# Two transformer-like blocks on one core: rope by pairs of heads, the delta rule's moment, low halves and rope tables in another order

## The chip, the cores and the metric

One core of a Trainium2 chip runs the whole program. The metric is the device time in microseconds. The kernel before took 2430.34 us (median of 3 runs, 2429.22 to 2437.76). The profiled execution took 2433.86 us, with a span of 2432.1 us from the first to the last instruction.

## The reference

The program computes a first block of 2 layers (l = 0, 1) and then a second block of 2 layers on an input of 256 rows by 1024 columns, all in float32. Cut to what the change touches:

```python
# first block, each layer: FFN, mixer, FFN (four FFNs, f0 to f3)
h = modulated_norm(x, norm_g[l, 0], sh1, sc1)
x = x + 0.5 * g1 * ((silu(h @ wg) * (h @ wu)) @ wd)        # D_FF = 2816
m = attn_pool_mixer(...) if l % 2 == 0 else short_conv_mixer(...)

# second block, each layer: FFN, hybrid mixer, FFN
cos, sin = rope_tables(positions)     # ang = positions[..., None] * 10000 ** (-arange(32) / 32)
proj = x @ w_in                       # feeds three branches and the gates
# DeltaNet branch: o = gated_delta_rule(...); o = rms_norm(o, norm_w) * silu(z); then @ w_o
# convolution branch: causal depthwise convolution of 31 taps on 512 channels, layer norm, @ w_pw2
# latent attention branch:
q = (rms_norm(c_q, q_norm_w) @ w_uq).reshape(b, t, 4, 128 + 64)   # 4 heads, 128 plain + 64 for rope
q_rope = apply_rope(q[..., 128:], cos, sin)
k_rope = apply_rope(k_r, cos, sin)    # one for all heads
s = (q_nope @ k_nope.T + q_rope @ k_rope.T) * scale               # causal, by blocks of 128
def apply_rope(x, cos, sin):          # x1, x2: the two halves of 64
    return concatenate([x1 * cos - x2 * sin, x2 * cos + x1 * sin])
```

## The kernel before

The kernel is written engine by engine: each engine has its own list of work, in the order of its code, and waits on named semaphores for the others. Nothing is scheduled by a planner; the order of the code is the order of the work.

**Weights.** They stream from memory as chunks of 128x2048 float32 (1 MB) into a ring of 5 buffers, loaded by SyncE. A product in float32 precision is made as three fast ones: ScalarE rounds a chunk to its high half (`w_hi`, line 1807), VectorE subtracts it to get the low half (`w_lo`, line 2281), and TensorE does high x high, low x high and high x low (lines 942 to 944). VectorE converts one chunk ahead of the use (`LEAD = 1`). `convert()` does one chunk, `ahead(n)` all up to chunk n.

**An FFN** runs over 11 strips of 256 columns of its hidden width. For each, `pair(i)` on TensorE: gate and up products (24 matmuls of 512 columns), the hidden rows turned by TensorE, 24 more matmuls of gate and up, then 24 that take the turned hidden rows down. For that the turned rows are also split: ScalarE rounds them (`hid_hi`, line 1875), VectorE makes the low half (`hid_lo`, line 2304, in `hid_rest`), and TensorE's down products wait for it. In the FFNs of the first block, f0 to f3, VectorE also accumulates the modulation vectors (`ada`, lines 2399 to 2409) from `w_ada`, which GpSimd's queue loads. Second-block FFNs have no such work.

**The rope tables** are computed once. In the kernel before this happens in the short convolution mixer of the first block (around 800 to 826 us): `rope_angles` on VectorE (lines 2769 to 2783) for 64 partitions, sine and cosine on ScalarE (lines 2032, 2033), then `rope_cosines` (2787, 2789).

**The hybrid mixer** of the second block (twice: around 1223 to 1535 us and 1922 to 2235 us). In the stretch that the change touches TensorE does, in this order: the delta rule's last products; half of a projection (`proj(20)`); the sums of squares of the delta output (line 1146, 16 matmuls of one column); the other half of the projection; `head_rows` (line 1152), which waits until the inverse roots are there (`hd_rstd`, a power on GpSimd, line 740, of the moment that VectorE makes at line 2587); the rope part of the queries (line 1669, 12 matmuls); the products of the delta branch (`branch(0, ...)`, which need `y_lo` from VectorE); `proj(21)`; then, after a wait for `branch_free`, the plain part of the queries and keys (lines 1689, 1694); `proj(22)`; and the rope rotation (lines 1700, 1701). VectorE meanwhile fills its gaps with taps of the convolution (`taps(n)`, line 2890: n rounds of 3 instructions; GpSimd does a fourth share, lines 912, 916), and it scales the delta output (3027, 3031), makes `y_lo` (2304) and `merged` (3040), which gives `branch_free`. A float32 matmul that isn't split (line 1669 for one) counts as two passes in the profile: x24 stands for 12 matmuls.

## Time and profile before

| | |
|---|---|
| median of 3 runs | 2430.34 us |
| profiled execution | 2433.86 us, span 2432.1 us |
| TensorE (PE) busy | 2354.2 us, 97% |
| VectorE (DVE) busy | 1622.1 us, 67% |
| ScalarE (ACT) busy | 1083.9 us, 45% |
| GpSimd (POOL) busy | 310.5 us, 13% |
| mean granted TensorE clock | 0.985 |

Times in the rows are microseconds from the span's start. A row of the timeline gives start, duration, engine, line, operation, what it writes and reads, how many instructions are merged, and in brackets how long the engine had been idle before it and who ended that. TensorE's clock is granted at full (1.0, 2.4 GHz) or half (0.5, 1.2 GHz); a stretch's PEclk is the mean of that.

### The profile page before, as it was taken

What the parts mean: (1) busy time and instruction counts of PE and PEld (TensorE: products, weight loads), DVE (VectorE), ACT (ScalarE), POOL (GpSimd) and SP (SyncE); (2) the same over time, 40 slices, a digit from 0 to 9 for tenths busy, and PEclk for the clock granted to TensorE, in tenths of its full rate; (3) what the DMA queues carried; (4) which work ended last, traced back from release to release, by engine and by line L of the source; (5) the groups of instructions that cost most, each with busy time, mean ns of one, the idle gap of its engine ahead of it and who ended that gap; (6) DMA issues with size and microseconds to landing.
All of it is one profiled execution on the core that took longest, in us unless ns stands there. A gap on an engine that the chain in (4) does not pass through costs nothing.

```text
span 2432.1 us, 32250 instructions
## 1 busy us (share of the span) xinstructions
PE 2354.2 (97%) x13225; PEld 2006.2 (82%) x13225; DVE 1622.1 (67%) x1799; ACT 1083.9 (45%) x1256; POOL 310.5 (13%) x419
## 2 busy tenths in 40 slices
PE   5999999999999999999999999999999999999998
PEld 4787868887878888888899889788788899888887
DVE  6998557768886765655576776745654666858544
ACT  3444554445335544344364335434344455344442
POOL 3110201101103000010003800000100007400000
PEclk9999999999999999999999899999999999999999
DMA  9996429868975576555654234556456442434653
GB/s 330 360 336 225 139 95 316 302 221 300 314 260 175 183 236 199 187 179 188 213 155 131 90 105 148 183 190 223 158 190 225 139 144 80 141 122 156 208 188 123
DMA packets 330461, 477.62 MB, mean 196 GB/s; under 512 B 19835, under 2 KB 267994, under 8 KB 330314
## 3 DMA queue, kind: packets, MB, share of 16 engines
q1 hardware_dynamic: 307514, 396.33, 49.6%
q0 software_dynamic: 22800, 79.23, 9.0%
q8 instruction: 104, 1.70, 0.3%
q14 instruction: 43, 0.35, 0.1%
HBM read 474.45 MB, written 1.05 MB: 196 GB/s over the span
## 4 chain that ended last, share of the span: by engine, by line
PE 66%; DVE 10%; issue 7%; POOLq 5%; DMA 4%; ACT 3%; DVEq 3%; POOL 1%; SPq 0%; ACTq 0%
PE ps L942 20%; PE ps L944 20%; PE ps L943 20%; DVE w_lo L2281 4%; DMA raw<-in_ffn_wu_dram 3%; POOLq L913 3%; POOLq L917 2%; ACT w_hi L1807 2%; DVE mix_mem L2401 1%; PE ps L1017 1%; DVEq L2417 1%; DMA probs<-in_w_ada_dram 1%; DVE parts L2370 1%; POOL n_rstd L746 1%; DVE mix_mem L2906 1%
## 5 line engine op out<-in xcount | busy, mean ns | idle before, releaser
L2281 DVE TENSOR_TENSOR w_lo<-raw,w_hi 128x2048 fp32r<-128x2048 f32 (+2 forms) x374 | 823.5, 2203 | 381.1 <-ACT w_hi L1807 376.5
L1807 ACT ACTIVATE w_hi<-raw 128x2048 fp32r<-128x2048 f32 (+2 forms) x368 | 687.0, 1868 | 471.0 <-PE ps L944 170.3
L942 PE MATMUL ps<-w_hi,x_hi 128*128 128x512 f32 x1504 | 598.6, 398 | 12.6 <-DVE x_lo L2304 8.4
L944 PE MATMUL ps<-w_hi,x_lo 128*128 128x512 f32 x1504 | 588.4, 391 | 0.0
L943 PE MATMUL ps<-w_lo,x_hi 128*128 128x512 f32 x1504 | 587.2, 390 | 0.0
L942 PEld LDWEIGHTS ps<-w_hi,x_hi 128*128 128x128 f32 x1504 | 283.3, 188 | 71.8 <-issue 10.5
L944 PEld LDWEIGHTS ps<-w_hi,x_lo 128*128 128x128 f32 x1504 | 283.2, 188 | 60.9
L943 PEld LDWEIGHTS ps<-w_lo,x_hi 128*128 128x128 f32 x1504 | 283.8, 189 | 56.7 <-issue 0.5
L942 PE MATMUL ps<-x_hi,w_hi 128*128 128x256 f32 (+1 forms) x992 | 290.1, 292 | 0.1
L943 PE MATMUL ps<-x_lo,w_hi 128*128 128x256 f32 (+1 forms) x992 | 284.7, 287 | 0.0
L944 PE MATMUL ps<-x_hi,w_lo 128*128 128x256 f32 (+1 forms) x992 | 284.7, 287 | 0.0
L942 PE MATMUL ps<-w_hi,hid_hi 128*128 128x512 f32 x640 | 252.2, 394 | 9.1 <-DVE hid_lo L2304 8.8
L944 PE MATMUL ps<-w_hi,hid_lo 128*128 128x512 f32 x640 | 249.2, 389 | 0.0
L943 PE MATMUL ps<-w_lo,hid_hi 128*128 128x512 f32 x640 | 249.1, 389 | 0.0
L942 PEld LDWEIGHTS ps<-x_hi,w_hi 128*128 128x128 f32 (+1 forms) x992 | 193.9, 195 | 1.0 <-issue 0.8
L943 PEld LDWEIGHTS ps<-x_lo,w_hi 128*128 128x128 f32 (+1 forms) x992 | 193.8, 195 | 0.7 <-issue 0.5
L944 PEld LDWEIGHTS ps<-x_hi,w_lo 128*128 128x128 f32 (+1 forms) x992 | 193.6, 195 | 0.0
L1875 ACT ACTIVATE hid_hi<-ps 128x512 fp32r<-128x512 f32 (+1 forms) x96 | 53.8, 561 | 257.8 <-PE ps L1017 257.8
L746 POOL TENSOR_TENSOR n_rstd<-n_moment,half_neg 128x1 f32<-128x1 f32 x24 | 22.4, 933 | 1133.3 <-DVE n_moment L2374 910.2
L942 PEld LDWEIGHTS ps<-w_hi,hid_hi 128*128 128x128 f32 x640 | 120.1, 188 | 39.3 <-issue 10.7
L1870 ACT ACTIVATE silu_g<-ps 128x256 f32<-128x256 f32 x176 | 65.9, 381 | 181.5 <-PE ps L944 180.9
L943 PEld LDWEIGHTS ps<-w_lo,hid_hi 128*128 128x128 f32 x640 | 120.1, 188 | 25.6 <-issue 1.2
(415 smaller groups left out, 2833.7 us busy)
## 6 DMA issues: line engine op xcount, KB each, us to landing
raw<-in_w_in_dram SPq DMA_DIRECT2D x96, 512.0 KB, 4.8
raw<-in_ffn_wg_dram SPq DMA_DIRECT2D x88, 512.0 KB, 4.7
raw<-in_ffn_wu_dram SPq DMA_DIRECT2D x88, 512.0 KB, 6.1
raw<-in_ffn_w_gate_dram SPq DMA_DIRECT2D x88, 512.0 KB, 4.0
raw<-in_ffn_w_up_dram SPq DMA_DIRECT2D x88, 512.0 KB, 5.1
raw<-in_ffn_wd_dram SPq DMA_DIRECT2D x80, 512.0 KB, 5.2
raw<-in_ffn_w_down_dram SPq DMA_DIRECT2D x80, 512.0 KB, 4.2
spare<-in_w_ada_dram POOLq DMA_DIRECT2D x40, 512.0 KB, 6.0
```

The costliest lines, as they stand in the source:

```text
L746: g.tensor_tensor(n_rstd[:, t:t + 1], n_moment[:, t:t + 1], half_neg[:, 0:1], ALU.pow)\
L913: pool.drain()
L917: pool.drain()
L942: pe.matmul(dst, wh, vh, start=start, stop=False, skip_group_check=True)
L943: pe.matmul(dst, wh, vl, start=False, stop=False, skip_group_check=True)
L944: return pe.matmul(dst, wl, vh, start=False, stop=stop_, skip_group_check=True)
L1017: last = pe.transpose(ps[:, 2, at_:at_ + P], hid[:, at_:at_ + P], ident[:])
L1807: return f(w_hi[at.hi_slot()][:, cols], raw[at.raw_slot()][:, cols], ACT.Copy)
L1870: f(silu_g[:, t * T:t * T + T], ps[:, gu_bank(i, t), 0:T], ACT.Silu).then_inc(gate_read, 1)
L1875: f(hid_hi[:, t0:t0 + n, :, :], ps[:, 2, 2 * P * t0:2 * P * (t0 + n)] .rearrange("p (t k n) -> p t k n", t=n, k=2), ACT.Copy).then_inc(hid ...
L2281: return v.tensor_tensor(w_lo[s][:, cols], raw[s][:, cols], w_hi[at.hi_slot()][:, cols].bitcast(F32), ALU.subtract)
L2370: v.bn_stats(parts[:, t, half, :], xt[:, t, cols])
```

## The change

Four edits, independent of each other:

1. **Rope by pairs of heads.** The tables, the rotation matrix and the keys' rope part are laid out on 128 partitions instead of 64 (the same 64 rows twice), and the queries' rope part of two heads stands in one tile of 128 partitions. The product that makes it (line 1669) has 6 matmuls of 128 rows in place of 12 of 64, the rotation 1 of 512 columns in place of 2. For the scores the keys are kept in two tiles, each with one half zeroed (`k_halves`, two more memsets on VectorE), so that a pair's tile gives the score of one head. To have the weights in that order, `w_uq` is loaded by 6 DMAs in place of 1, in pieces of 128 and 64 columns. ScalarE copies the keys' part twice.
2. **The delta moment sooner.** In the hybrid mixer VectorE makes the moment right after a conversion, without `taps(2)` ahead of it, and then waits for GpSimd's power before it goes on (`head_scales` in place of `head_scales_begin`). The two rounds of taps come later, ahead of `merged`.
3. **Low halves sooner.** In f0 to f3 `hid_rest(1)` stands ahead of a conversion and of a step of `ada`, and at the end of the FFN `hid_rest(n)` ahead of the last conversion.
4. **Rope tables later.** `rope_angles` and `rope_cosines`, with the sine and cosine on ScalarE, move from the short convolution mixer into f3, the FFN behind it.

```diff
-        rot = sb("rot", [64, P])
-        cos_t = sb("cos_t", [64, T])
+        rot = sb("rot", [P, P])
+        cos_t = sb("cos_t", [P, T])
...
-        q_rope = shaped(flat(out_sb)[0:64, :], (HEADS, T))
+        q_rope = shaped(flat(out_sb)[:, 0:2 * T], (2, T))
+        k_halves = low[:, 0:2, :]
...
-                sp.dma_start(uq[:, :, :], a["mla_w_uq_2"][l:l + 1].rearrange("o (k p) n -> p (o k) n", p=P))\
-                    .then_inc(mla_uq, 16)
+                w_uq = a["mla_w_uq_2"][l].rearrange("(k p) (h n) -> p k h n", p=P, h=HEADS)
+                for k in range(3):
+                    sp.dma_start(uq[:, k, 0:512].rearrange("p (h n) -> p h n", h=HEADS), w_uq[:, k, :, 0:P])\
+                        .then_inc(mla_uq, 16)
+                    sp.dma_start(uq[:, k, 512:768].rearrange("p (h n) -> p h n", h=HEADS), w_uq[:, k, :, P:192])\
+                        .then_inc(mla_uq, 16)
...
-                for h in range(HEADS):
+                for i in range(2):
                     for k in range(3):
-                        last = pe.matmul(ps[0:64, 6 + h // 2, T * (h % 2):T * (h % 2) + T],
-                                         uq[:, k, 192 * h + P:192 * h + 192], low[:, k, :], start=(k == 0), stop=(k == 2))
+                        last = pe.matmul(ps[:, 6, T * i:T * i + T], uq[:, k, 512 + P * i:512 + P * i + P], low[:, k, :],
+                                         start=(k == 0), stop=(k == 2))
...
-                for i in range(2):
-                    pe.matmul(ps[:, 4 + i, :], rot[:], q_rope[:, 2 * i:2 * i + 2, :], start=True, stop=True)
+                pe.matmul(ps[:, 4, :], rot[:], q_rope[:], start=True, stop=True)
...
-                    pe.matmul(dst, q_rope[:, h, P * b:P * b + P], k_rope[:, 0:P * (b + 1)], start=False, stop=False,
+                    pe.matmul(dst, q_rope[:, h // 2, P * b:P * b + P], k_halves[:, h % 2, 0:P * (b + 1)], start=False, stop=False,
...
+                    if f_no == 3 and i == 4:
+                        act.wait_ge(rope_conv, 1)
+                        f(sin_t[:], angle, ACT.Sin)
+                        f(cos_t[:], angle, ACT.Sin, scale=0.5).then_inc(rope_sin, 1)
...
+                    if i == 1:
+                        hid_rest(1, (0, 1))
                     convert()
                     ada(grp, steps[1])
-                    hid_rest(i, (0, 1))
+                    if i > 1:
+                        hid_rest(i, (0, 1))
...
+                if grp is None:
+                    ahead(b + FFN_CH)
+                hid_rest(n, (0, 1))
                 ahead(b + FFN_CH)
-                hid_rest(n, (0, 1))
...
-                taps(2)
-                head_scales_begin(call_h(l, 2), 3, 8, 1.0 / P, B_EPS)
+                head_scales(call_h(l, 2), 3, 8, 1.0 / P, B_EPS)
                 ahead(n0 + 23)
                 taps(1)
...
                 ahead(n0 + 25)
-                taps(4)
+                taps(6)
```

`head_scales` is `head_scales_begin` followed by a wait of VectorE on `hd_rstd`, which GpSimd gives when its power is done.

VectorE in the hybrid mixer, first layer of the second block, from a conversion of `proj(20)`'s stretch to the delta branch's `y_lo`, before (line 2890 is a tap):

```order
L2281 TENSOR_TENSOR w_lo<-raw_49,w_hi 128x2048 [waits hi_ready]
L2890 SCALAR_TENSOR_TENSOR diag<-probs,cols,diag 128x243 x2
L2890 SCALAR_TENSOR_TENSOR diag<-probs,cols,diag 128x250
L2890 SCALAR_TENSOR_TENSOR diag<-probs,cols,diag 128x242 x2
L2890 SCALAR_TENSOR_TENSOR diag<-probs,cols,diag 128x249
L2587 TENSOR_SCALAR moment<-ps 128x8 [waits hd_stats]
L2281 TENSOR_TENSOR w_lo<-raw_50,w_hi 128x2048 [waits hi_ready]
L2890 SCALAR_TENSOR_TENSOR diag<-probs,cols,diag 128x241 x2
L2890 SCALAR_TENSOR_TENSOR diag<-probs,cols,diag 128x248
L3027 SCALAR_TENSOR_TENSOR work<-out_sb,cols,ps 128x512 [waits hd_rows]
```

And the same place in the changed kernel, with the rows that now stand behind `y_lo`:

```order
L2286 TENSOR_TENSOR w_lo<-raw_49,w_hi 128x2048 [waits hi_ready]
L2601 TENSOR_SCALAR moment<-ps 128x8 [waits hd_stats]
L2286 TENSOR_TENSOR w_lo<-raw_50,w_hi 128x2048 [waits hi_ready,hd_rstd]
L2900 SCALAR_TENSOR_TENSOR diag<-probs,cols,diag 128x243 x2
L2900 SCALAR_TENSOR_TENSOR diag<-probs,cols,diag 128x250
L3036 SCALAR_TENSOR_TENSOR work<-out_sb,cols,ps 128x512 [waits hd_rows]
L3040 TENSOR_TENSOR work<-work,spare 128x512
L3036 SCALAR_TENSOR_TENSOR work<-out_sb,cols,ps 128x512
L3040 TENSOR_TENSOR work<-work,spare 128x512
L2309 TENSOR_TENSOR y_lo<-work,y_hi 128x512 [waits y_hi_ready] x2
L2286 TENSOR_TENSOR w_lo<-raw_51,w_hi 128x2048 [waits hi_ready]
L2286 TENSOR_TENSOR w_lo<-raw_52,w_hi 128x2048 [waits hi_ready]
```

The moment has moved ahead of two rounds of taps (6 instructions), the conversion behind it has a second wait, and the 6 tap instructions stand behind the two conversions at the end.

VectorE at the end of f2, the third FFN of the first block, before (`y_lo` is here the low half of the last down weights, `mix_mem` the modulation):

```order
L2409 TENSOR_REDUCE mix_mem<-mix_mem 128x32
L2437 TENSOR_TENSOR mix_mem<-mix_mem,ps 128x512 [waits gate_mm,gate_in]
L2281 TENSOR_TENSOR w_lo<-raw_51,w_hi 128x2048 [waits hi_ready]
L2304 TENSOR_TENSOR y_lo<-work,y_hi 128x2048 [waits d_hi_ready]
L2281 TENSOR_TENSOR w_lo<-raw_52,w_hi 128x2048 [waits hi_ready]
L2304 TENSOR_TENSOR hid_lo<-ps,hid_hi 128x512 [waits hid_hi_ready]
L2465 SCALAR_TENSOR_TENSOR hid<-silu_g,ps 128x256 [waits gate_read]
```

And in the changed kernel:

```order
L2414 TENSOR_REDUCE mix_mem<-mix_mem 128x32
L2442 TENSOR_TENSOR mix_mem<-mix_mem,ps 128x512 [waits gate_mm,gate_in]
L2286 TENSOR_TENSOR w_lo<-raw_51,w_hi 128x2048 [waits hi_ready]
L2309 TENSOR_TENSOR y_lo<-work,y_hi 128x2048 [waits d_hi_ready]
L2309 TENSOR_TENSOR hid_lo<-ps,hid_hi 128x512 [waits hid_hi_ready]
L2286 TENSOR_TENSOR w_lo<-raw_52,w_hi 128x2048 [waits hi_ready]
L2470 SCALAR_TENSOR_TENSOR hid<-silu_g,ps 128x256 [waits gate_read]
```

One conversion has gone from ahead of `hid_lo` to behind it.

## Rows read from the trace of the kernel before

**Rows 1.** Waits of PE: engine, line, releaser: us in total, times, longest.
```profile
PE ps L942 <- DVE hid_lo L2304: 13.5, 11, 2.5
...
PE ps L1152 <- POOL rstd L740: 5.2, 2, 2.6
```

**Rows 2.** Timeline, PE, four FFN places: f0, f1, f2, end of f2.
```profile
69.23 0.47 PE L942 MATMUL ps<-w_hi,hid_hi 128*128 128x512 f32 x1 [2.48 <-DVE hid_lo L2304]
...
378.81 0.47 PE L942 MATMUL ps<-w_hi,hid_hi 128*128 128x512 f32 x1 [1.09 <-DVE hid_lo L2304]
...
571.44 0.47 PE L942 MATMUL ps<-w_hi,hid_hi 128*128 128x512 f32 x1 [0.69 <-DVE hid_lo L2304]
...
724.17 0.47 PE L942 MATMUL ps<-w_hi,hid_hi 128*128 128x512 f32 x1 [2.22 <-DVE hid_lo L2304]
```

**Rows 3.** Chain of waits in f0, start, us, what; then VectorE's timeline, end of f2.
```profile
67.20 1.28 DVE mix_mem L2401
...
721.13 2.29 DVE L2281 TENSOR_TENSOR w_lo<-raw,w_hi 128x2048 fp32r<-128x2048 f32 x1
```

**Rows 4.** Stretch 100 to 120: engines' busy us (PE, PEld, DVE, ACT, POOL), PEclk, DMA, GB/s.
```profile
100.00:120.00 20.00, 19.99 (x90) 16.25 (x89) 18.00 (x15) 8.78 (x8) 3.85 (x7) 1.00 1.04 387
```

**Rows 5.** Timeline, short convolution mixer: ACT, DVE and PE; then DVE in f3.
```profile
814.60 0.58 ACT L2026 ACTIVATE mix_mem<-ps 128x512 f32<-128x512 f32 x1
...
815.28 0.69 DVE L2798 TENSOR_TENSOR mix_mem<-mix_mem,ps 128x512 f32<-128x512 f32 x1 [1.34 <-ACT mix_mem L2026]
...
821.07 0.47 PE L942 MATMUL ps<-w_hi,y_hi 128*128 128x512 f32 x1 [1.58 <-DVE w_lo L2281]
...
926.71 0.69 DVE L2304 TENSOR_TENSOR hid_lo<-ps,hid_hi 128x512 fp32r<-128x512 f32 x1 [2.21 <-ACT hid_hi L1875]
```

**Rows 6.** Timeline, PE, hybrid mixer.
```profile
1382.21 0.41 PE L942 MATMUL ps<-x_hi,w_hi 128*128 128x256 f32 x1
...
1389.44 1.97 PE L1152 MATMUL ps<-ident,rstd 128*128 128x128 f32 x8 [2.62 <-POOL rstd L740]
...
1397.29 0.39 PE L942 MATMUL ps<-y_hi,w_hi 128*128 128x256 f32 x1
...
1415.47 0.70 PE L1689 MATMUL ps<-mix_mem 128*128 128x256 f32 x2 [0.65 <-DVE mix_mem L3040]
```

**Rows 7.** Timeline, POOL: hybrid mixer, then two other powers, in the first block.
```profile
1381.02 2.03 POOL L916 TENSOR_TENSOR diag<-diag,silu_g 128x230 f32<-128x230 f32 x1
1385.73 3.65 POOL L740 TENSOR_TENSOR rstd<-moment,half_neg 128x8 f32<-128x8 f32 x1 [2.68 <-DVE moment L2587]
...
326.48 1.01 POOL L740 TENSOR_TENSOR rstd<-moment,half_neg 128x4 f32<-128x4 f32 x1 [35.28 <-DVE moment L2587]
...
278.76 2.92 POOL L740 TENSOR_TENSOR rstd<-moment,half_neg 128x16 f32<-128x16 f32 x1 [16.52 <-DVE moment L2587]
```

**Rows 8.** Timeline, DVE, hybrid mixer.
```profile
1382.52 2.89 DVE L2890 SCALAR_TENSOR_TENSOR diag<-probs,cols,diag 128x243 f32<-128x243 f32 x6
...
1391.45 0.75 DVE L3027 SCALAR_TENSOR_TENSOR work<-out_sb,cols,ps 128x512 f32<-128x512 f32 x1 [2.44 <-PE ps L1152]
...
1394.71 1.76 DVE L2304 TENSOR_TENSOR y_lo<-work,y_hi 128x512 fp32r<-128x512 f32 x2
...
1402.93 5.14 DVE L2890 SCALAR_TENSOR_TENSOR diag<-probs,cols,diag 128x240 f32<-128x240 f32 x12
...
1412.93 2.48 DVE L3040 TENSOR_TENSOR mix_mem<-mix_mem,ps 128x512 f32<-128x512 f32 x4
```

**Rows 9.** Chain of waits, hybrid mixer: start, us, what.
```profile
1415.47 5.45 PE ps L1689 x24
...
1430.11 1.91 PE ps L1700 x4
```

**Rows 10.** Stretch 1382 to 1387, columns as in rows 4.
```profile
1382.00:1387.00 5.00, 4.82 (x28) 4.61 (x27) 4.85 (x9) 0.00 (x0) 2.32 (x2) 0.66 0.86 272
```

**Rows 11.** DMA issues 1365 to 1385: KB each, median us to landing.
```profile
mix_mem<-in_mla_w_uq_dram SPq DMA_DIRECT2D x1, 1152.0 KB, 5.4
```

More of the change, by code:

```diff
@@ L210, in block_kernel @@
         low = carve(5, T)
[L211 removed]
+        k_rope = carve(T)
         gate = carve(KT, T)
@@ L237, in block_kernel @@
         q_nope = work[:, 0:4, :]
-        q_rope = shaped(flat(out_sb)[0:64, :], (HEADS, T))
-        rot_q = shaped(flat(spare)[0:64, :], (HEADS, T))
-        rot_k = weights[0:64, :]
+        q_rope = shaped(flat(out_sb)[:, 0:2 * T], (2, T))
+        rot_q = shaped(flat(spare)[:, 0:2 * T], (2, T))
+        rot_k = weights[:]
+        k_halves = low[:, 0:2, :]
         par = flat(out_sb)
@@ L249, in block_kernel @@
         level_tmp = weights[:, 0:P]
-        count_b = weights[0:64, P:P + 1].bitcast(I32)
-        pos_i, angle, turns_f = flat(spare)[0:64, 0:T].bitcast(I32), probs[0:64, 0, 0, :], probs[0:64, 0, 1, :]
-        rope_k = probs[0:64, 1, 0, :].bitcast(I32)
+        count_b = weights[:, P:P + 1].bitcast(I32)
+        turns = shaped(mix_mem[:, 5 * D:5 * D + 4 * T], (4, T))
+        pos_i, angle, turns_f, rope_k = turns[:, 0, :].bitcast(I32), turns[:, 1, :], turns[:, 2, :], turns[:, 3, :].bitcast(I32)
         ps = keep.enter_context(nc.psum_tensor("ps", [P, 8, 512], F32))
@@ L859, in _ @@
                 pool.drain()
-            for half in range(2):
+            for half in range(4):
                 pool.drain()
@@ L2131, in mix_b @@
                         chunk_done(n0 + 5)
-                        f(k_rope[:], ps[0:64, 3, 0:T], ACT.Copy)
+                        for half in range(2):
+                            f(k_rope[64 * half:64 * half + 64, :], ps[0:64, 3, 0:T], ACT.Copy)
                         f(kr_ab, ps[0:KR_AB, 3, 0:T], ACT.Copy).then_inc(kr_out, 1)
@@ L2519, in ffn @@
                         count = (total - late) * i // (n - 1) - (total - late) * (i - 1) // (n - 1)
+                        if f_no == 3 and i == 4:
+                            rope_angles()
+                        if f_no == 3 and i == 6:
+                            rope_cosines()
                         pair(i, tuple((count + part) // 4 for part in (3, 1, 2, 0)), gates if i == n - 1 else 0)
@@ L3047, in mix_b @@
                 dve.wait_ge(rot_mm, l + 1)
-                v.tensor_tensor(rot_q[:], ps[0:64, 4:6, :].rearrange("p b (k n) -> p (b k) n", k=2),
-                                bc(sin_t[:].unsqueeze(1), (64, HEADS, T)), ALU.mult)
-                v.tensor_tensor(rot_k, ps[0:64, 3, 0:T], sin_t[:], ALU.mult)
-                v.tensor_tensor(q_rope[:], q_rope[:], bc(cos_t[:].unsqueeze(1), (64, HEADS, T)), ALU.mult)
+                v.tensor_tensor(rot_q[:], ps[:, 4, :].rearrange("p (k n) -> p k n", k=2),
+                                bc(sin_t[:].unsqueeze(1), (P, 2, T)), ALU.mult)
+                v.tensor_tensor(rot_k, ps[:, 3, 0:T], sin_t[:], ALU.mult)
+                v.tensor_tensor(q_rope[:], q_rope[:], bc(cos_t[:].unsqueeze(1), (P, 2, T)), ALU.mult)
                 v.tensor_tensor(k_rope[:], k_rope[:], cos_t[:], ALU.mult)
+                v.memset(k_halves[64:P, 0, :], 0.0)
+                v.memset(k_halves[0:64, 1, :], 0.0)
                 dve.drain()
                 v.tensor_tensor(q_rope[:], q_rope[:], rot_q[:], ALU.add)
-                v.tensor_tensor(k_rope[:], k_rope[:], rot_k, ALU.add).then_inc(rope_done, 1)
+                v.tensor_tensor(k_halves[0:64, 0, :], k_rope[0:64, :], rot_k[0:64, :], ALU.add)
+                v.tensor_tensor(k_halves[64:P, 1, :], k_rope[64:P, :], rot_k[64:P, :], ALU.add).then_inc(rope_done, 1)
                 ahead(n0 + 29)
```

30 lines of the change are left out of this document (11 added, 19 removed).

## The prediction

> **What bounds the kernel now.** I read the page's busy shares first: TensorE works 2354.2 of 2432.1 us, 97%, at a mean clock of 0.985. So an edit counts only if it takes work off TensorE or shortens one of its pauses, and all pauses with thin stretches hold some 78 us. Next come the waits of PE, which say who ends the pauses: VectorE's `hid_lo` ends 13.5 us of them in 11 waits, and GpSimd's power 5.2 us in 2 [rows 1]. Then PE's timeline, for where these are: of the hid_lo waits four are near the change, at 69.23, 378.81, 571.44 and 724.17, with 2.48, 1.09, 0.69 and 2.22 us [rows 2]. In the hybrid mixer PE stands 2.62 us before the head rows, and 0.65 us before line 1689 [rows 6]; the second mixer repeats this within 0.5 us. Last, at each pause, the timelines of VectorE, GpSimd and ScalarE, for what the late engine did just before.
>
> **Low halves sooner.** In the strip behind 69.23 VectorE's order was a conversion of 2.29 us, a step of `ada` of 1.28 us, and then `hid_lo`; the step starts at 67.20 and is the one on the chain of waits [rows 3]. With `hid_lo` ahead of both, 3.57 us leave the front of it, more than the wait of 2.48. What is late next is the conversion, for TensorE's next products. VectorE's work isn't smaller, and it has little air here: from 100 to 120 us it is busy 18.00 of 20, while the DMA engines are busy all the time, 387 GB/s [rows 4]. An FFN that is bound by what the queues bring gives an early gain back at the next chunk. Bounds: 0 (all given back) and -2.5. I take -0.7, near the lower gain, since the row of 100:120 is the nearest one to how f0 goes on. For f1 (1.09) the same exchange stands further from the start of the weights' stream, and I take all of it, -1.1 (bounds 0 and -1.1); for f2 (0.69) -0.4 (0 and -0.7). At the end of f2 one conversion of 2.29 us [rows 3] leaves the front of `hid_lo`, and the wait of 2.22 us [rows 2] goes: -2.2 (0 and -2.2). The conversion that moves behind is the last of the FFN, needed by a later chunk only. At the other strips and ends nothing waits, so there it brings 0. Sum: -0.7 - 1.1 - 0.4 - 2.2 = -4.4.
>
> **Rope tables later.** In the short convolution mixer PE stands 1.58 us at 821.07 for a conversion. VectorE had been late since 815.28, where it waited 1.34 us for ScalarE's line 2026 [rows 5], which stood in ScalarE's list behind the sine and cosine that themselves wait for VectorE's angles. Without them ScalarE comes about 1 us sooner, and the wait shrinks by as much: -1.0 (0 and -1.6). In f3, where they go, some 4 us of VectorE's work are added over two strips, against idle times such as the 2.21 us before `hid_lo` at 926.71 [rows 5]; each strip lasts about 14 us and has more than one such hole. I cost them at 0. Without that cover they would cost their length, 4 us at most.
>
> **The hybrid mixer: the moment.** The sums that the moment reads are made on PE by 1382.21, where the second half of `proj(20)` starts [rows 6]. VectorE spends 2.89 us on six taps from 1382.52 [rows 8], and the power starts at 1385.73, takes 3.65 us, and PE goes on at 1389.44 [rows 6, 7]. Now the moment comes at about 1382.6. GpSimd is at its own tap until 1383.05 (1381.02 + 2.03), so the power starts at 1383.1. How long it takes with VectorE waiting for it, no row shows: powers of 4 and 16 columns took 1.01 and 2.92 us, which gives 1.01 + 4/12 x 1.91 = 1.65 for 8, and the one of 8 columns itself took 3.65, beside a conversion [rows 7]. I take 1.65, because the changed order has VectorE standing idle meanwhile; ends: 1.0 and 3.65. So the power is done at 1384.75, ahead of PE's end of the chunk (1389.44 - 2.62 = 1386.82): the pause of 2.62 us goes.
>
> A price for it stands on VectorE: it waits from 1382.7 to 1384.75, and behind it are queued the conversion and every later one. Its list then runs: conversion 2.28, three taps 1.3, line 3027 [rows 8]. So line 3027 starts at 1384.9 + 2.2 + 1.3 = 1388.4 or, if PE's head rows come later, with them: these start at 1386.85, and VectorE needs the first bank only. I take 1388.3, against 1391.45: 3.15 sooner.
>
> The Trainium skill (page "SBUF — State Buffer", section "Who interferes with whom") has a rule on this: VectorE with two inputs in SBUF and a GpSimd instruction that reads SBUF exclude each other for a whole instruction. The rows agree with it (3.65 beside a conversion, where 1.65 would be in line with the other two). By the rule the power alone takes 1.65; by the row of 8 columns taken as it is, 3.65, which is the slower rival below.
>
> **The queries' rope part.** Line 1669 goes from 12 matmuls of 64 rows to 6 of 128 with the same 256 columns. PE spends on them what lies between the head rows' end (1389.44 + 1.97 = 1391.41) and 1397.29 [rows 6], 5.88 us for 24 passes; half of it is 2.9, at 5.45/24 = 0.227 us a pass as on line 1689 [rows 9] it is 2.7. I take 2.7. PE is then through with it at 1386.82 + 1.97 + 2.7 = 1391.5 at the latest, and up to 1.3 sooner where the clock is full in the head rows; but the branch needs `y_lo`. Its first half stands at 1394.71 + 0.9, 4.15 us behind line 3027 [rows 8], so now at 1388.3 + 4.15 = 1392.4. PE starts the branch at 1392.4 in place of 1397.29 (4.9 sooner), after a new pause of 0.9 to 2.2 us.
>
> **Where it is lost.** From 1397.29 to the end of `proj(21)` at 1415.47 - 0.65 = 1414.82 PE works 17.53 us [rows 6]; now it ends at 1409.9. But line 1689 needs `branch_free`, given by the second of the `merged` instructions of line 3040 that start at 1412.93 [rows 8]; PE went on at 1415.47. From line 3027 at 1391.45 to there are 24.0 us, filled with conversions, taps (12 in 5.14 us [rows 8]) and two idle times of together 1.55 us before conversions. The six taps that were moved (2.89 us at the start, 5.14/12 x 6 = 2.57 at this place) now stand inside this chain. So line 1689 may start at 1388.3 + 24.0 + 2.57 = 1414.9, 0.6 sooner than before; with the idle times shorter, up to 1.1. I take -0.8. In one sentence: VectorE has the same work from the moment to `merged` as before, its wait for the power (2.1 us) stands in place of its wait for the head rows (2.44 us, rows 8), and PE's gain of 4.9 us turns into a pause of 4 to 4.5 us before line 1689.
>
> Such pauses have a second price. After the one-column sums PE's chunk from 1382.21 took 4.61 us, with a granted clock of 0.66 in that stretch [rows 10]: part of it at 1.2 GHz in place of 2.4. At full clock it is 0.66 x 4.61 = 3.04, so 1.57 was lost. I add 1.5 per mixer for the stretch behind the long pause; bounds 0 and 3.1 (two such stretches, one after each new pause).
>
> **The rotation** has 2 passes fewer of the 4 that took 1.91 us [rows 9]: -0.9. Per mixer -0.8 + 1.5 - 0.9 = -0.2, for two -0.4.
>
> **Costed at nothing.** The six DMAs of `w_uq`: the one took 5.4 us to land [rows 11], and is needed at 1391.4 [rows 6], 22 us after its issue at 1369; even four times that is hidden, though its runs are now 512 and 256 bytes. The second copy of the keys on ScalarE (about 0.4 us), the memsets, and the rope on VectorE, which covers the same elements on twice the partitions, lie behind PE's products of `proj(22)`. The scores' matmuls have 128 rows in place of 64 at the same columns: 0.
>
> **Sum.** -4.4 - 1.0 - 0.4 = -5.8 us against the profiled 2433.86: 2428.1. The runs' median is 3.5 lower than that execution, so 2424.5 for the runs.
>
> **Rivals.**
> 1. The clock stays up and VectorE's idle times shrink: each mixer gives 0.8 + 0.9 = 1.7, at both 3.4 in place of 0.4, total -8.8: 2421.5. For it: ahead of 1382 stood matmuls of one column, and ahead of the new pauses stand full ones. Against: any pause of some us may do the same, and this mixer's first one is followed by a slow stretch.
> 2. VectorE's chain doesn't hold line 1689, and PE's shorter list counts in full: 2.6 + 2.7 + 0.9 = 6.2, and up to 8 a mixer with the slow start at 1382 better covered; at 8 the total is -5.4 - 16 = -21.4: 2409. Against it: the 0.65 us before line 1689 [rows 6] shows the chain already as the one that ends last.
> 3. First-block gains are given back because queues and VectorE are full [rows 4]: -0.7, -1.1 and -0.4 fall out, and 1.4 of the 2.2: -2.2 is left: 2428.1.
> 4. Slower: the power takes 3.65 us even alone, and VectorE stands 4.1 us for it. Line 3027 starts at 1390.3 and line 1689 at 1416.9 less 0.6, 0.9 later than before; two slow stretches add 3.1, the rotation gives 0.9: +3.1 a mixer, +6.2 with both. With the first block's -5.4 that is +0.8: 2431.1. It decides from the point where line 1689, measured from PE's 1382.21, starts 0.5 us later than before with two slow stretches behind it, or 2.1 with one (5.4/2 + 0.9 less 3.1 or 1.5). For it: the only row of this shape. Against: the other two powers.
> 5. The edits don't do what they say: `hid_lo` waits for ScalarE's `hid_hi`, not for VectorE's list. Against: the chain of waits in f0 goes through the `ada` step [rows 3]. It would give the time of rival 3.
>
> **How the numbers follow.** Forecast 2424.5: 0.50. Rival 1: 0.18. Rival 2: 0.07. Rivals 3 and 5 together: 0.12. Rival 4: 0.13. The range 2417 to 2431 leaves out rival 2 and half of rival 4, with the ends of rival 1: about 0.18. A measurement of this kernel tells a change from none at about 0.5%, which is 12 us: faster is below 2418.2, slower above 2442.5. Faster holds rival 2 and the lower end of rival 1: 0.13. Slower needs rival 4 with lost cover in f3 (4 us) and more: 0.03. Same: 0.84.
>
> **What would show it.** Right: no pause before the head rows; a power of 8 columns near 1.65 us; a new pause of 0.9 to 2.2 us for `y_lo` and one of 4 to 4.5 us before line 1689's place with `mix_mem` as releaser; the four waits of rows 2 gone or under 0.3; the wait at 821 near 0.6; f3 as long as before. Wrong: PE's new pause before line 1689 under 2 us (rival 2), a power of over 3 us (rival 4), new waits for `w_lo` in f0 and f1 (rival 3), a clock of 1.0 behind the pauses (rival 1).

## The result and the profile after

The changed kernel took 2414.69 us (median of 4 runs, 2411.86 to 2418.54) against 2429.78 for the kernel before; the ratio is 0.9942, with a 95% interval of 0.9919 to 0.9964. Timed again in 10 runs it gave 2414.84 us, ratio 0.9942 [0.9923, 0.9962]. The forecast was 2424.5 with a range of 2417 to 2431: the sign was right, the size was not, and the result lies below the range. The gain is 15 us where 5.8 were forecast.

The profiled execution took 2411.86 us, with a span of 2410.1 us, so against the profiled execution before (2433.86) it shows 22 us. Some of that belongs to the two executions and not to the kernels: the profiled one lies 3.5 us above the median before and 2.8 us below it after. It has to be taken out first (runs before_again and shifted, below).

The waits of PE in the changed kernel, in the columns of [rows 1]:

```profile
PE ps L948 <- DVE y_lo L2309: 7.4, 3, 4.0
PE ps L948 <- DVE x_lo L2309: 6.8, 4, 4.8
PE ps L1695 <- DVE mix_mem L3049: 6.1, 2, 3.1
...
PE ps L948 <- DVE hid_lo L2309: 4.7, 4, 1.3
```

The wait before the head rows is gone. In its place stand 6.5 us for `y_lo` (2.51 and 4.01, the third of the row is in the first block) and 6.1 us for `merged`, two new waits a mixer. `hid_lo` ends 4.7 us of pauses in place of 13.5, but waits for the product `hid` at the same line have grown from 0.3 to 3.8 us (2.21, 1.01 and 0.57 in f0, f1 and f2). The hybrid mixer on PE's timeline, which answers to [rows 6]:

```profile
1374.35 1.03 PE L1158 MATMUL ps<-ident,rstd 128*128 128x128 f32 x8
1375.22 2.76 PE L1675 MATMUL ps<-mix_mem 128*128 128x256 f32 x12
1380.49 0.55 PE L948 MATMUL ps<-y_hi,w_hi 128*128 128x256 f32 x1 [2.51 <-DVE y_lo L2309]
...
1402.47 5.45 PE L1695 MATMUL ps<-mix_mem 128*128 128x256 f32 x24 [2.99 <-DVE mix_mem L3049]
```

And VectorE and GpSimd there, which answer to [rows 7, 8]:

```profile
1370.23 0.15 DVE L2601 TENSOR_SCALAR moment<-ps 128x8 f32<-128x8 f32 x1
1372.60 2.29 DVE L2286 TENSOR_TENSOR w_lo<-raw,w_hi 128x2048 fp32r<-128x2048 f32 x1 [2.22 <-POOL rstd L745]
...
1376.63 0.75 DVE L3036 SCALAR_TENSOR_TENSOR work<-out_sb,cols,ps 128x512 f32<-128x512 f32 x1
```

```profile
1368.73 2.03 POOL L922 TENSOR_TENSOR diag<-diag,silu_g 128x230 f32<-128x230 f32 x1
1370.89 1.67 POOL L745 TENSOR_TENSOR rstd<-moment,half_neg 128x8 f32<-128x8 f32 x1
```

The power took 1.67 us alone (1.65 forecast, 3.65 before), VectorE waited 2.22 us for it (2.1 forecast), PE stood 2.51 us for `y_lo` and 2.99 us for `merged`. In the second mixer the pauses are 4.01 and 3.15 us: there PE's chunk behind the one-column sums ran at a clock of 1.00, where the first had 0.61, and PE came to the wait for `y_lo` 1.5 us sooner.

To place the rest I measured the hybrid mixer in stretches, from PE's timelines. Zero is the start of the delta's one-column sums (line 1146 before). The stretches are: the start of the plain part of the queries (line 1689 before), the start of the rotation (1700), from there to the convolution's sums (1713), from these to the first score (1724), and from the first score to the next transposes of x (971):

| us | 1689 at | 1700 at | to the sums | to first score | scores to transposes | whole |
|---|---|---|---|---|---|---|
| before, mixer 1 | 35.07 | 49.64 | 11.63 | 13.61 | 77.61 | 152.5 |
| before, mixer 2 | 34.72 | 49.29 | 11.63 | 13.53 | 77.62 | 152.1 |
| after, mixer 1 | 34.37 | 48.85 | 10.48 | 11.99 | 75.25 | 146.6 |
| after, mixer 2 | 34.37 | 48.86 | 10.48 | 11.99 | 75.25 | 146.6 |

So a mixer is 5.7 us shorter on average: 0.4 to 0.7 at line 1689, 1.15 in the rotation, 1.6 between the sums and the scores, and 2.37 in the scores. The last two are what the prediction did not have.

The scores themselves, PE's timeline before:

```profile
1455.28 0.46 PE L1724 MATMUL ps<-mix_mem,work 128*128 128x128 f32 x2 [0.58 <-ACT mix_mem L2109]
1455.67 0.48 PE L1726 MATMUL ps<-mix_mem,out_sb 64*128 64x128 f32 x2
1456.08 0.23 PE L1171 MATMUL ps<-cmask_b,ident_b 128*128 128x128 bf16 x1
1456.15 0.44 PE L1724 MATMUL ps<-mix_mem,work 128*128 128x128 f32 x2
```

And after, from the second score on (here and below, the rows of a score's product are the partitions it sums over, 64 or 128):

```profile
1439.99 0.44 PE L1729 MATMUL ps<-mix_mem,work 128*128 128x128 f32 x2
1440.27 0.39 PE L1731 MATMUL ps<-mix_mem,out_sb 128*128 128x128 f32 x2
1440.49 0.22 PE L1177 MATMUL ps<-cmask_b,ident_b 128*128 128x128 bf16 x1
1440.55 0.44 PE L1729 MATMUL ps<-mix_mem,work 128*128 128x128 f32 x2
```

Before, a score's round takes 1456.15 - 1455.28 = 0.87 us, after it 1440.55 - 1439.99 = 0.56. The merged rows of the trace give the same busy time for both products within about 0.1 us; the difference is in the starts. Going from 128 rows to 64 and back costs 0.3 us a score, eight scores a mixer. The four scores of 256 columns lose the same 0.29 us as the four of 128 (from its first product to its mask 1.15 us before, 0.86 after), so the cost goes with the change and not with the columns. The whole stretch of the scores took 77.61 or 77.62 us in every profiled mixer with 64 rows but one (in score64, below), and 75.24 to 75.29 in every one with 128.

### The profile page after: what moved, and what is told of

It is laid out like the page before. It is cut to its first block, busy times and chain, and to the rows that moved or that the text cites. A ratio compares the mean times of both kernels' runs of the same rounds, so it can differ in the third digit from the quotient of the medians.

```text
span 2410.1 us, 32218 instructions
## 1 busy us (share of the span) xinstructions
PE 2333.2 (97%) x13197; PEld 2000.3 (83%) x13197; DVE 1620.1 (67%) x1805; ACT 1083.9 (45%) x1258; POOL 313.7 (13%) x421
## 4 chain that ended last, share of the span: by engine, by line
PE 72%; DVE 8%; issue 6%; POOLq 5%; ACT 3%; DVEq 2%; DMA 2%; POOL 1%; SPq 0%; ACTq 0%
PE ps L948 22%; PE ps L950 22%; PE ps L949 22%; POOLq L919 3%; DVE w_lo L2286 3%; POOLq L923 2%; PE ps L1023 1%; ACT w_hi L1812 1%; DMA raw<-in_ffn_wu_dram 1%; DVE diag L2900 1%; DVE mix_mem L2406 1%; DVE parts L2375 1%; POOL n_rstd L751 1%; DVEq L2422 1%; DVE mix_mem L2916 1%
```

## The experiments

**The four edits one by one.** Each is the kernel before with one edit of the diff. They shared 34 runs of the kernel before (2430.77 us).

*pairs*: edit 1 alone (the tables stay in the short convolution mixer).

```diff
-    for h in range(HEADS):      # 4 x 3 matmuls, 64 rows of output
+    for i in range(2):          # 2 x 3 matmuls, 128 rows
-    pe.matmul(dst, q_rope[:, h, ...], k_rope[:, ...])                 # 64 rows
+    pe.matmul(dst, q_rope[:, h // 2, ...], k_halves[:, h % 2, ...])   # 128 rows
```

> The kernel before with the rope by pairs of heads alone. Theory A (the rope part of a score on 64 rows costs TensorE a change of shape each time, 0.3 us for each of 16 scores): each score of 128x128 goes from 0.86 to 0.56 us, -4.8 us for the program, and the rotations another -2.1; the queries' rope part is 2.7 us shorter per mixer, which turns into a wait for y_lo. Total -7 us, 2422.8 against 2429.8; up to -10 if the one-column sums of the convolution (line 1713 before) also run at full clock. Rival B (the scores are shorter in the changed kernel only because the clock or the phase of the stretch differed): the score's steps stay at 0.86 us when nothing else moves, total -2 us.

Measured: 2418.69 us, ratio 0.9950 [0.9935, 0.9965], 12.1 us faster. The scores took 75.25 and 75.28 us in place of 77.6, the rotation's stretch 10.48, the sums' stretch 11.99 and 10.50. In the first mixer line 1695 came at 34.66, after a wait of 1.55 us. Theory A holds, and one edit of the four carries most of the gain; it is more than the 7 to 10 us that the theory allowed.

*moment*: edit 2 alone.

```diff
-    taps(2)
-    head_scales_begin(call_h(l, 2), 3, 8, 1.0 / P, B_EPS)
+    head_scales(call_h(l, 2), 3, 8, 1.0 / P, B_EPS)
...
-    taps(4)
+    taps(6)
```

> The kernel before with the delta moment sooner alone. Theory A (VectorE's chain up to merged binds): the power of 8 columns takes 1.67 us, the wait at the head rows goes, the branch starts 3.9 us sooner, and line 1689 only 0.6 to 0.8 us sooner, after a wait of 3 us for mix_mem. Total -1.4 us (2428.4). Rival B (TensorE's own list binds): line 1689 2.6 us or more sooner in each mixer, total -5 us or more.

Measured: 2435.87 us, ratio 1.0022 [1.0008, 1.0035], so 5.1 us slower. Neither theory has that. VectorE, GpSimd and PE in its first mixer:

```profile
1378.28 0.15 DVE L2587 TENSOR_SCALAR moment<-ps 128x8 f32<-128x8 f32 x1
1382.53 2.29 DVE L2281 TENSOR_TENSOR w_lo<-raw,w_hi 128x2048 fp32r<-128x2048 f32 x1 [4.10 <-POOL rstd L740]
```

```profile
1376.78 2.11 POOL L916 TENSOR_TENSOR diag<-diag,silu_g 128x231 f32<-128x231 f32 x1
1379.06 0.87 POOL L912 TENSOR_SCALAR silu_g<-probs,cols 128x230 f32<-128x230 f32 x1 [0.17 <-issue]
1380.08 0.59 POOL L916 TENSOR_TENSOR diag<-diag,silu_g 128x230 f32<-128x230 f32 x1
1380.82 1.68 POOL L740 TENSOR_TENSOR rstd<-moment,half_neg 128x8 f32<-128x8 f32 x1
```

```profile
1412.81 7.48 PE L1689 MATMUL ps<-mix_mem 128*128 128x256 f32 x24 [4.88 <-DVE mix_mem L3039]
```

Two things add up. GpSimd was one round of its own taps (231, then 230 columns) further back, so VectorE waited 4.10 us and not 2.22; line 1689 came at 36.63 us after the sums in place of 35. And behind the pause of 4.88 us the 24 passes of line 1689 took 7.48 us, where they took 5.45 [rows 9]; the granted clock from 1412 to 1420 is 0.69 (after, 1402 to 1410: 1.00):

```profile
1412.00:1420.00 8.00, 7.19 (x24) 6.03 (x25) 7.71 (x15) 0.84 (x2) 0.00 (x0) 0.69 0.05 17
```

Some 1.5 us come back further on: from the sums to the first score both mixers took 12.02 us, where the first profile before had 13.5.

*low*: edit 3 alone (its first half is shown; the end of each FFN is as in the diff above).

```diff
+    if i == 1:
+        hid_rest(1, (0, 1))
     convert()
     ada(grp, steps[1])
```

> The kernel before with the low halves sooner alone. Theory A (the wait in the first strip moves from hid_lo to hid, since the product hid stands behind the same conversion and ada step): f0 and f1 keep their length; the wait of 2.48 us is replaced by one of 2.2 for hid, the 1.09 by 1.0; only the end of f2 gives 2.2 to 2.5 us. Total -2.5 to -3.5 us (2427). Rival B (hid_lo's place alone sets the first strip): -4.4 us and no wait for hid.

Measured: 2427.83 us, ratio 0.9991 [0.9975, 1.0007], 2.9 us faster and within the noise. By the ratio the gain is 2.2 us. In f0 the wait is now for the product `hid`:

```profile
71.64 0.50 PE L942 MATMUL ps<-w_hi,hid_hi 128*128 128x512 f32 x1 [2.19 <-DVE hid L2465]
```

The wait of 2.22 us at the end of f2 is gone, with no other in its place. Theory A. f1 shows the first strip best: from its first transposes to those of f2 PE took 193.51 and 193.48 us in the two profiles of the kernel before, 193.78 here and 193.47 in the changed kernel, where 1.1 less was forecast. f0, measured likewise up to its mixer, can't show it: it took 187.68 and 191.26 us in two executions of the same kernel.

*tables*: edit 4 alone.

```diff
+    if f_no == 3 and i == 4:
+        rope_angles()
+    if f_no == 3 and i == 6:
+        rope_cosines()
```

> The kernel before with the rope tables in the third FFN's follower f3 alone (64 partitions). Theory A: the wait of 1.58 us in the short convolution mixer goes altogether and f3 keeps its length: -1.6 us (2428.2). Rival B: it comes back in f3 as waits of hid_lo or hid near pairs 4 to 7: 0.

Measured: 2430.04 us, ratio 1.0000 [0.9984, 1.0016]. In the trace the wait of 1.58 us is gone (the mixer is 1.67 us shorter than before), and f3 is no longer; the time doesn't resolve 1.6 us. Its first hybrid mixer, whose code is untouched, took 10.51 us from the sums to the first score in place of 13.5.

**What carries the gain, taken from the changed kernel.** These four shared 17 runs of the kernel before (2430.89 us).

*score64*: the rope part of a score over 64 rows. Both heads of a pair then take the rope rows of the first one, so the second head's own are left out.

```diff
-    pe.matmul(dst, q_rope[:, h // 2, ...], k_halves[:, h % 2, ...])
+    pe.matmul(dst, q_rope[0:64, h // 2, ...], k_halves[0:64, 0, ...])
```

> The changed kernel, with the rope part of each score taken over the 64 lower rows alone (both heads of a pair read the same rows, so part of the scores is left wrong). Theory A (a product over 64 rows between products over 128 costs TensorE a change of shape, about 0.3 us a score): each of 16 scores 0.3 us longer, total +4.8 us against the changed kernel's 2414.7, so 2419.5 (0.9955 of before). Rival B (the number of rows is free and the shorter scores came from the clock): the scores keep 0.56 us, no difference.

Measured: 2424.19 us, ratio 0.9972 [0.9960, 0.9983]. PE's timeline shows the old spacing with everything else as after (1452.63 - 1451.76 = 0.87 us a score):

```profile
1451.76 0.46 PE L1729 MATMUL ps<-mix_mem,work 128*128 128x128 f32 x2 [0.58 <-ACT mix_mem L2113]
1452.15 0.49 PE L1731 MATMUL ps<-mix_mem,out_sb 64*128 64x128 f32 x2
1452.57 0.23 PE L1177 MATMUL ps<-cmask_b,ident_b 128*128 128x128 bf16 x1
1452.63 0.44 PE L1729 MATMUL ps<-mix_mem,work 128*128 128x128 f32 x2
```

The first mixer's score stretch is 77.62 us again, 2.37 more. That settles the scores: 4.7 us for the program. The time is up by 9.5 by the medians and by 7.3 by the ratios, more than that. The one profiled execution has more delays that could be the rest, and these come and go with the same code (strip1_undone has the first one too): in the first mixer VectorE waited 5.98 us for a power that stood two rounds of taps back (line 1695 came 3.7 us later), and slow stretches of 1.4 and 1.5 us fell one behind line 1695, one into the second mixer's scores (79.11 us). How much of the 9.5 they are on average isn't shown.

*late_taps*: four rounds of taps from ahead of `merged` to behind it, where the last call of `taps` makes all that are left.

```diff
     ahead(n0 + 25)
-    taps(6)
+    taps(4)
     ahead(n0 + 26)
-    taps(2)
```

> The changed kernel with four of the eight rounds of taps between y_lo and merged moved behind merged. Theory A (VectorE's chain up to merged holds line 1695): 12 tap instructions, 5.1 us, leave the chain, the waits of 3.0 and 3.15 us before line 1695 go, total -6 us, 2408.7 (0.991 of before); the sums of the convolution then may wait for the taps by up to 2 us a mixer, which would leave -2. Rival B (line 1695 waits for TensorE's own products through another path): no change.

Measured: 2418.61 us, ratio 0.9944 [0.9925, 0.9964]: no gain. The waits before line 1695 went and it came at 31.2 us, 3.2 sooner. But PE then waited 1.99 us at the convolution's sums for VectorE's last rope addition, and the stretch from the sums to the score took 13.7 us in place of 12.0. The chain up to `merged` does hold line 1695, and behind it stands the next one of VectorE, which took 2.1 of the 3.2 us back. The other 1.7 us went in the stretch behind, at a clock of 0.75; whether the moved taps or the place in time made that isn't shown.

*made_sooner*: the first `hid` ahead of the second conversion in the first strip. For that strip the order becomes:

```diff
     hid_rest(1, (0, 1))
     convert()
-    ada(grp, steps[1])
-    convert()
     made(i, 0)
+    convert()
+    ada(grp, steps[1])
```

> The changed kernel with the first product hid of the first strip of f0 to f3 ahead of the second conversion, and the ada step behind both. Theory A (the wait of the first strip is now for hid, and its place behind a conversion and an ada step makes it): the waits for hid of 2.2, 1.0 and 0.6 us go; f1 and f2 are 1.0 and 0.6 us shorter, f0 up to 2.2: total -2 to -3.8 us, 2411.8 (0.992 of before). Rival B (the weights' stream or the conversions set the pace of the first strips): the waits turn into waits for w_lo, total 0.

Measured: 2414.67 us, ratio 0.9926 [0.9907, 0.9944]. The waits of 2.2, 1.0 and 0.6 us for `hid` are gone from the trace. f1 came out 1.24 us shorter (192.23); f0 has a wait of 1.12 us for `hid_lo` one strip later, and f2 one of 1.87 us. The time can't tell it from the changed kernel.

*no_moment*: the changed kernel without edit 2.

```diff
-    head_scales(call_h(l, 2), 3, 8, 1.0 / P, B_EPS)
+    taps(2)
+    head_scales_begin(call_h(l, 2), 3, 8, 1.0 / P, B_EPS)
```

> The changed kernel with the moment and the taps where they were before (three of the four edits). Theory A (moved alone the moment cost 5 us, since VectorE's chain gives 0.3 us a mixer back and the longer pause is followed by a slow stretch; with the rope by pairs it is worth about nothing): 2414 to 2418, line 1695 after a wait of 1.5 us. Rival B (the moment's gain of 2.6 us a mixer becomes real once the queries' rope part is short): 2420 or more. Rival C (it costs here as it does alone): 2410.

Measured: 2415.46 us, ratio 0.9932 [0.9911, 0.9953]. PE waits 4.67 and 4.11 us for the power, and line 1695 comes at 34.49 and 34.66 us: 0.1 to 0.3 later than in the changed kernel. Beside the other edits the moment is worth nothing that the time resolves. The three edits alone gave -12.1, -2.9 and -0.7 us, together -15.7; in one kernel they give -15.4.

**The moment's wait.** With 15 runs of the kernel before (2430.86 us).

> The changed kernel once more, timed in as many rounds as its variants beside it. Every theory: 2414.7, between 2412 and 2419, if the first 4 runs stood for it.

*after_again* gave 2414.84 us (above), and both mixers 146.56 us, as the first profile.

*power_sooner*: GpSimd's power one round of taps sooner.

```diff
-    if sh == 27:
+    if sh == 26:
         head_power(call_h(l, 2), 8)
```

> The changed kernel with GpSimd's power of the delta moment one round of its own taps sooner. Theory A (VectorE waits for the power as long as GpSimd is behind with its taps: 2.2 us when one tap product is left, 4.1 when one more round is, as in the run of the moment alone): VectorE's wait is 1.8 us or less in both mixers whatever the phase, line 1695 comes 0.4 to 2 us sooner after the sums than 34.4 us; total -1 to -4 us against the changed kernel. Rival B (the power's own 1.67 us and the conversion behind it set the chain): no change.

Measured: 2417.36 us, ratio 0.9940 [0.9920, 0.9961]. In the first mixer VectorE's wait fell to 1.78 us and `y_lo` came 0.5 us sooner, but line 1695 did not (34.57); in the second it was 2.32. That is less than theory A asked, and the time doesn't show its gain. PE's pause before line 1695 grew to 3.62 and 3.35 us, and the second was followed by a slow stretch:

```profile
2100.54 8.30 PE L1695 MATMUL ps<-mix_mem 128*128 128x256 f32 x24 [3.35 <-DVE mix_mem L3049]
```

*moment_no_wait*: VectorE doesn't wait for the power.

```diff
-    head_scales(call_h(l, 2), 3, 8, 1.0 / P, B_EPS)
+    head_scales_begin(call_h(l, 2), 3, 8, 1.0 / P, B_EPS)
```

> The changed kernel with VectorE going on to the conversion behind the moment, without the wait for the power. Theory A (the wait of 2.2 us lies in VectorE's chain up to merged, which binds): the power takes 3.6 us beside the conversion, the head rows start about when TensorE's chunk ends, and line 1695 comes 1 to 2.2 us sooner; total -2 to -4 us. Rival B (the power beside a conversion is what the wait protects from): a pause of 1 to 2 us at the head rows comes back and y_lo is later, total 0 to +2.

Measured: 2417.62 us, ratio 0.9937 [0.9914, 0.9960]. In the first mixer the power took its 1.67 us, but started 4.4 us behind the moment, since GpSimd's tap beside the conversion had grown from 0.9 to 2.71 us; PE waited 3.3 us at the head rows again. Line 1695 came at 35.23 and 33.40, after pauses of 4.63 us both times, and both were followed by slow stretches. Rival B in one mixer, theory A in the other, and in this execution the slow stretch (2.7 and 3.0 us) took back more than the gain; 1.5 us of it came back before the scores (10.5 us in place of 12.0).

*three_and_made*: no_moment and made_sooner together.

> The changed kernel with the moment and its taps where they were before, and with the product hid of the first strip sooner (rope by pairs, low halves, tables, hid). Theory A (the moment sooner brings nothing, and the first strip's wait is one for hid): 2412 to 2415, as fast as the changed kernel or up to 2 us faster. Rival B (the moment's edit carries part of the gain): 2418 or more.

Measured: 2411.86 us, ratio 0.9917 [0.9894, 0.9939], the best of all, 3 us below the changed kernel beside it (0.9942 [0.9923, 0.9962]). The intervals overlap, so that it beats the changed kernel is likely and not shown. With no_moment it says that leaving edit 2 out costs nothing that these runs resolve.

**What was left open.** With 23 runs of the kernel before (2431.40 us).

*strip1_undone*: `hid_rest(1)` back behind the conversion and the ada step.

```diff
-    if i == 1:
-        hid_rest(1, (0, 1))
     convert()
     ada(grp, steps[1])
-    if i > 1:
-        hid_rest(i, (0, 1))
+    hid_rest(i, (0, 1))
```

> The changed kernel with hid_rest(1) of f0 to f3 back behind the conversion and the ada step; the end of each FFN stays changed. Theory A (the edit only renames the wait, from hid_lo to hid): 2414.8, within 1.5 us of the changed kernel; a wait of 2.3 us for hid_lo in f0 in place of 2.2 us for hid, 1.0 in f1 and 0.6 in f2. Rival B (the edit gives what was predicted, 2.2 us in all): 2417.

Measured: 2420.07 us (6 runs, 2414.43 to 2422.03), ratio 0.9941 [0.9922, 0.9959], against 0.9942 for the changed kernel. By the ratio nothing; by its median, which both theories put lower, it is 5 us above that of the changed kernel, which was not timed beside it. The profiled execution shows what such a difference can be made of: in the first mixer VectorE waited 5.97 us for the power and line 1695 came 3.6 us later, and in both mixers the work behind the pause before line 1695, no longer than in the changed kernel, ran slow and took 2.8 us more.

```profile
1411.02 8.28 PE L1695 MATMUL ps<-mix_mem 128*128 128x256 f32 x24 [2.96 <-DVE mix_mem L3046]
```

None of that touches f0 to f3. There the trace has 2.47 us for `hid_lo` in f0 where the changed kernel has 2.21 for `hid`, 0.94 in f1 for 1.01, 0.52 in f2 for 0.57. f1 took 193.36 us and f2 190.66, against 193.47 and 190.68 in the changed kernel. In f1 and f2 the edit renames the wait and gives nothing. f0 took 4.6 us more here, but with the same code it differed by 3.6 us in the two profiles of the kernel before, so there only the waits can be compared.

*shifted*: 1.7 us more of rotation ahead of the convolution's sums.

```diff
-    for i in range(2):
+    for i in (0, 0, 0, 1):
         pe.matmul(ps[:, 4 + i, :], rot[:], q_rope[:, 2 * i:2 * i + 2, :], start=True, stop=True)
```

> The kernel before with the first rotation product of the queries made three times in place of once, in each hybrid mixer: two more products of 512 columns on 64 rows, 1.9 us of TensorE's time more per mixer ahead of the convolution's sums. By its length alone: +3.8 us, 2434.7. Theory A (the clock's drop behind the one-column sums depends on when they fall, not on what the changed kernel does in them): from the sums' start (line 1713) to the first score it takes 12.0 or 10.5 us in at least one mixer, in place of 13.5, total 2431 to 2434. Rival B (it depends on the work around the sums alone): 13.5 us in both mixers, 2434.7.

Measured: 2433.59 us, ratio 0.9999 [0.9983, 1.0016]. The stretch to the sums grew from 11.63 to 13.35 us in both mixers, and the one behind it, whose code is untouched, fell from 13.5 to 11.99 and 11.98 us. Theory A. The run shows one thing more. Its rotation products over 64 rows stand in a row, and the two more took 0.86 us each (3.70 us against 1.98 for line 1700), as much as the same product over 128 rows takes in the changed kernel (0.86 us from line 1705 to line 1706). So 64 rows aren't slower by themselves; the change of rows is what costs.

*before_again*: the kernel before.

> The kernel before once more, for a second profile. Theory A (the two waits of 0.9 us in f2 at 606 and 675 us, and the 13.5 us from the sums to the first score, are of that one execution): at least one of the two differs. Rival B (they belong to the kernel): both are there again.

Measured: 2431.87 us, ratio 0.9995 [0.9979, 1.0010]. The second mixer took 12.02 us from the sums to the first score where the first profile had 13.53 (the first mixer has 13.53 again), and the waits of 0.9 us in f2 at 606 and 675 us are not there. Theory A.

## Why the prediction was right and wrong

Two steps failed and make most of the miss. The scores with 128 rows in place of 64 were costed at 0 and gave 4.7 us. The clock was costed at +1.5 us a mixer behind the long pause; there it cost nothing, and a stretch that the sum doesn't have gave 1.6 us a mixer. Each term in turn:

**Low halves sooner, -4.4.** The end of f2 was right (2.2 forecast, the trace has 2.2 less in low). The first strips (-2.2 of the sum) were wrong, in f1 by measurement (193.5 us with and without the edit) and in f0 and f2 by the waits: the step "3.57 us leave the front of it, more than the wait" asked what stands ahead of `hid_lo`, and took the conversion as next. Next was `hid`, which stands behind the same conversion and ada step and for which PE waits halfway through the down products (2.21, 1.01 and 0.57 us). Rival 3 gave these terms up too, but because of full queues, and rival 5 because of ScalarE; neither is what the trace shows.

**Rope tables, -1.0.** The mechanism and the cover in f3 were right, and 1.67 us is the whole wait; I had taken off only what ScalarE's delay of 1 us explained.

**The moment.** The steps up to line 1689 came out nearly as forecast: the power 1.67, `y_lo` at 12.4 us after the sums against 16.9 (4.5 sooner, 4.9 forecast), line 1689 at 34.37 against 35.07 and 34.72 (-0.4 to -0.7; -0.8 forecast), VectorE as the bound. Rival 2 is out. The pause for `y_lo` was 2.51 and 4.01 us where 0.9 to 2.2 were forecast: in the first mixer `y_lo` came 0.4 us later than forecast, and in the second the chunk behind the sums ran at full clock. The pause before line 1689 is 3.0 and not 4 to 4.5, because the branch itself started in part at half clock (next point). What the prediction lacked is that VectorE's wait depends on GpSimd's place in its taps: 1.8 to 2.3 us, 4.1, or 5.98. Rival 4 had the right loser and a wrong cause, and alone the edit cost 5.1 us.

The Trainium skill (page "SBUF — State Buffer", section "Who interferes with whom") says that a VectorE instruction with two inputs in SBUF and a GpSimd instruction that reads SBUF contend for a port pair that only one of them can hold. The trace agrees: GpSimd's tap product took 0.59 us alone and 2.03 or 2.11 beside a conversion, and the power 1.67 and 3.65. So what GpSimd still has to do beside a conversion, and not the power's own length, sets when the power starts.

**The clock, +1.5 a mixer.** A slow stretch came, of the size forecast, and in a place where it costs nothing. Behind the pause of 2.51 us for `y_lo` the branch began at half clock:

```profile
1380.00:1388.00 8.00, 7.51 (x50) 7.54 (x51) 6.17 (x6) 5.05 (x6) 4.34 (x4) 0.79 0.01 3
```

From the branch's start to the end of `proj(21)` PE took 19.0 us (34.37 - 2.99 - 12.39) where it had taken 17.53, 1.5 more; but line 1689 waits for VectorE anyway, so this only shortened the pause. The step that failed is "I add 1.5 per mixer for the stretch behind the long pause": the work behind the pause before line 1695 ran at full clock in both profiles of the changed kernel, the sign that the prediction gave for rival 1. But rival 1's sum (1.7 us a mixer) doesn't fit either, and full clock there isn't a rule. Over the profiles of all kernels, of nine pauses of 2.96 to 3.15 us at this line three were followed by a slow stretch (1.4 to 2.8 us lost), of six of 3.35 to 4.89 us five were (2.0 to 3.0 us), and of 19 of under 2 us none was. So the slow stretch was more frequent behind a longer pause; what decides it in one execution stays open.

Instead of costing 1.5 there, the clock gave 1.6 in a stretch that I had not looked at, from the convolution's sums to the first score. But this stretch takes 13.5, 12.0 or 10.5 us with the same code in it (tables, shifted, before_again). Its work is the same each time and only the clock differs: 0.75 in the one of 13.61 us, 0.86 in one of 12.02, 1.00 in one of 10.51. So of the 3.1 us that the first two profiles show there, a part may be where in time the stretch fell. The gain of pairs by time (12.1) is larger than the steps that its trace fixes, (2.37 + 1.15 + 0.6) x 2 = 8.2 us, where 0.6 is the mean gain at line 1695, so on average some of it seems to be there.

The other profiles say the same. In the eight mixers of before, before_again, low and tables the stretch took 13.5 us six times, 12.0 once and 10.5 once, 13.0 on average. In the twenty of the ten kernels with edit 1, late_taps left out, it took 12.0 us twelve times, 10.5 eight times and 13.5 never, 11.4 on average. That is 1.6 us less a mixer, 3.2 in all. It goes with edit 1, though not with its number of rows, since shifted came to 12.0 with 64. Where the work behind line 1695 ran slow in these ten kernels, the stretch took 10.5 us in five of six mixers, elsewhere in three of fourteen. What it is in the timing that decides stays open.

**The rotation, -0.9.** Measured 1.15 a mixer: 0.86 for the product that is gone (shifted) and 0.29 that the sum hadn't, the switch from 128 rows to 64 and back, the same as in a score.

**The scores, "128 rows in place of 64 at the same columns: 0".** This is the largest error in a single step that an experiment fixes. It took the time of a matmul by its columns, and forgot what a change of the rows costs its neighbours. The trace of the kernel before had it: a score's round of 0.87 us for two products and a mask. The Trainium skill (page "TensorEngine Tiling (Array Packing)", section "Key Properties") says that changing the tiling mode drains TensorE. The page gives no figure, and no run shows that a plain product over 64 rows is such a mode; the 0.3 us for the way there and back in each score would fit it.

By terms: -4.7 for the scores, -6.2 for the clock (+3.0 forecast, -3.2 in the profiles), -0.5 for the rotation, -0.7 for the tables, +2.2 for the first strips and +0.5 for the moment (0.7 and 0.35 at line 1689 where twice 0.8 was forecast) make -9.4 beside the forecast -5.8, together -15.2, where -15.1 was measured. That it fits so well is in part luck: the terms are those of single profiles, and the clock's alone moves by 1.5 us from one execution to the next.

## What to carry to other kernels

Price a matmul with its neighbours: where a product over 64 rows stands alone among products over 128, padding it with zeros to 128 rows can be cheaper than leaving it small. When a wait is taken away, look for the second instruction behind the same obstacle; here it was 3 us further down VectorE's list. And a wait for GpSimd is as long as GpSimd's own list is late: read what stands ahead of the power on its timeline, not only the power.

## What the runs showed of the hardware

A float32 score of 128x128 took 0.56 us with both products over 128 rows and 0.87 with one of them over 64 (score64 against the changed kernel, nothing else changed), while products over 64 rows in a row took no longer than over 128 (shifted, 0.86 us each). TensorE's clock made steps of about 1.5 us in stretches with the same code: 10.5, 12.0 and 13.5 us from the convolution's sums to the first score; single profiles of this kernel differ by several such steps, so the difference of two profiled executions (22 us here, 15 by time) says little where each stretch isn't compared by itself. The granted clock around the stretch of 13.6 us before was 0.76, around the one of 12.0 in before_again 0.88, and around the one of 10.5 in tables 1.00:

```profile
1441.00:1455.00 14.00, 13.69 (x91) 13.45 (x90) 4.49 (x8) 3.34 (x5) 2.69 (x1) 0.76 0.25 76
```

```profile
2138.00:2152.00 14.00, 13.42 (x98) 12.72 (x97) 5.92 (x11) 5.29 (x8) 2.69 (x1) 0.88 0.35 100
```

```profile
1432.00:1444.00 12.00, 11.42 (x96) 10.98 (x94) 5.51 (x9) 4.38 (x6) 2.69 (x1) 1.00 0.32 91
```
